# Attention logits in a ring of three PSUM banks instead of two, and a 16-bit SBUF target for the output stage's squares

## The reference

```
h = rms_norm(x) * (1 + scale) + shift              # modulation from silu(c) @ w_ada
q_a,k_a,v_a,gate_a, q_i,k_i,w_i, q_b,k_b,v_b,gate_b = split(h @ w_in)
score = sum_h relu(q_i . k_i) * w_i                # indexer: top 256 keys of each query
o_a = softmax(q_a . k_a over the chosen keys) v_a  # 8 heads, 2 key heads, width 64
o_b = retention(q_b, k_b, v_b, state)              # 4 heads of 128
y = rms_norm(concat(o_a silu(gate_a), norm(o_b) silu(gate_b)) @ w_out)
x = x + gate * y
```

## Time and profile before

| | |
|---|---|
| median of 3 runs | 1569.04 us (1568.35 to 1569.26) |
| the profiled execution's own time | 1566.93 us |
| its span in the profile | 1565.1 us |
| mean granted TensorE clock | 0.971 |
| busy: PE, DVE, ACT, POOL | 91%, 67%, 50%, 24% |
| first attention stages (layer 0, layer 1) | about 460 to 715 us, 1217 to 1470 us |

### The profile page before, as it was taken

The page is one execution under the profiler, slowest core; times in us unless marked ns, Lnnn a source line. Parts: engine busy times, 40 slices in busy tenths (PEclk is TensorE's granted clock), DMA queues, the critical chain, the costliest instruction groups (busy, mean ns, idle before and its releaser), DMA issues.

```text
span 1565.1 us, 24314 instructions
## 1 busy us (share of the span) xinstructions
PE 1422.0 (91%) x7591; PEld 1073.2 (69%) x7591; DVE 1046.1 (67%) x3026; ACT 787.0 (50%) x1916; POOL 383.4 (24%) x350
## 2 busy tenths in 40 slices
PE   6869999999999799889965899999999988988996
PEld 1745777777887567557855658778788755755785
DVE  0686998999985446441366779999999654654224
ACT  2545665665236455554333466666632555545422
POOL 2540333334321001001234212434433100100110
PEclk9899999999999999999987999999999999999998
DMA  9312343332221112113332111211112210211324
GB/s 334 94 57 63 89 122 121 113 114 75 70 69 50 32 34 84 52 53 105 111 109 70 36 38 33 56 49 46 57 53 83 60 40 31 67 54 54 104 79 161
DMA packets 125190, 122.04 MB, mean 78 GB/s; under 512 B 33256, under 2 KB 94024, under 8 KB 125064
## 3 DMA queue, kind: packets, MB, share of 16 engines
q1 hardware_dynamic: 125064, 120.49, 25.3%
HBM read 93.55 MB, written 26.90 MB: 77 GB/s over the span
## 4 chain that ended last, share of the span: by engine, by line
PE 53%; DVE 29%; ACT 6%; issue 6%; DMA 3%; POOL 2%; SPq 1%; DVEq 0%; ACTq 0%
PE proj L902 10%; PE proj L903 10%; PE proj L905 9%; PE turn L881 8%; PE logit L921 6%; DVE U L1529 5%; PE out_bank L946 4%; DMA U<-x_dram 2%; DVE by_cos_sin L1467 2%; DVE U L1723 2%; DVE by_cos_sin L1469 2%; DVE turned L1484 1%; DVE score L1503 1%; DVE probsT_more L1602 1%; ACT probsT_more L1209 1%
## 5 line engine op out<-in xcount | busy, mean ns | idle before, releaser
L902 PE MATMUL proj<-w_hi,h_hi 128*128 128x512 f32 (+2 forms) x1440 | 582.5, 405 | 2.2 <-ACT U L1145 1.4
L903 PE MATMUL proj<-w_lo,h_hi 128*128 128x512 f32 (+2 forms) x1440 | 541.0, 376 | 0.0
L905 PE MATMUL proj<-w_hi,h_lo 128*128 128x512 f32 (+2 forms) x1280 | 482.9, 377 | 0.0
L1347 POOL TENSOR_TENSOR w_lo<-w_raw,w_hi 128x512 fp32r<-128x512 f32 (+2 forms) x160 | 206.7, 1292 | 839.1 <-ACT w_hi L1101 839.1
L902 PEld LDWEIGHTS proj<-w_hi,h_hi 128*128 128x128 f32 x1440 | 276.8, 192 | 62.3 <-issue 23.1
L903 PEld LDWEIGHTS proj<-w_lo,h_hi 128*128 128x128 f32 x1440 | 277.5, 193 | 31.4
L905 PEld LDWEIGHTS proj<-w_hi,h_lo 128*128 128x128 f32 x1280 | 244.6, 191 | 37.4
L1529 DVE TENSOR_SCALAR_CACHE_REDUCE U<-score,cand 128x384 bf16<-128x384 f32 x310 | 222.6, 752 | 2.2
L921 PE MATMUL logit<-keys,queries 64*128 64x512 f32 (+4 forms) x592 | 142.5, 557 | 40.8 <-DVE row_max L1673 22.7
L1209 ACT ACTIVATE probsT_more<-turn 128x512 f32<-128x512 f32 (+3 forms) x156 | 73.3, 491 | 159.6 <-PE turn L881 127.4
L881 PE MATMUL turn<-ident,U 128*128 128x128 f32 x696 | 114.9, 294 | 28.5 <-DVE U L1723 13.8
(11 more groups left out here) (154 smaller groups left out, 2025.6 us busy)
## 6 DMA issues: line engine op xcount, KB each, us to landing
w_raw<-in_w_in_dram SPq DMA_DIRECT2D x80, 256.0 KB, 3.2
probsT_more<-in_w_ada_dram SPq DMA_DIRECT2D x64, 256.0 KB, 3.8
score<-mixed_dram SPq DMA_DIRECT2D x36, 256.0 KB, 2.8
U<-in_x_prompt_dram SPq DMA_DIRECT2D x16, 512.0 KB, 4.1
score<-in_w_ada_dram SPq DMA_DIRECT2D x32, 256.0 KB, 5.0
w_raw<-in_w_out_dram SPq DMA_DIRECT2D x32, 256.0 KB, 3.2
mixed_dram<-U SPq DMA_DIRECT2D x24, 192.0 KB, 2.1
gates_dram<-U SPq DMA_DIRECT2D x18, 256.0 KB, 2.1
```

The costliest lines, as they stand in the source:

```text
L902: nc.tensor.matmul(out, h_hi[:, k, tile], hi, start=(k == 0), stop=False)
L903: ins = nc.tensor.matmul(out, h_hi[:, k, tile], lo, start=False, stop=(t == SAMPLE and k == KT - 1))
L905: ins = nc.tensor.matmul(out, h_lo[:, k, tile], hi, start=False, stop=(k == KT - 1))
L1347: nc.gpsimd.tensor_tensor(w_lo[:, s % WS, 0:w], w_raw[:, n % RAWS, 0:w], w_hi[:, s % WS, 0:w].bitcast(F32), ALU.subtract).then_inc(w_lo_re ...
```

## The change

The attention logits get a list and a ring of their own, with three banks: the two logit banks and `spare`. Indexer and retention logits keep the ring of two. Since the rings share banks, TensorE gets waits where a stage changes from one to the other: before the first attention logit of a layer, for the last two keys of the ring of two and for the last modulation copy, and before the first searched indexer tile of layer 1, for the last three keys of the ring of three. `Ring` counts by the number of its banks. The squares of the output groups and of the new x go to `square_dump`, 512 bf16 columns of one slot of `rows` in SBUF; those of the input tiles still go to `spare`.

```diff
--- before.py
+++ after.py
@@ -310,7 +310,10 @@
 
 TURNS, LOGITS = plan_units()
 TURN_AT = {key: n for n, key in enumerate(TURNS)}
+ATT_LOGITS = [key for key in LOGITS if key[0] == "l" and kind(key[1]) == "att"]
+LOGITS = [key for key in LOGITS if key not in set(ATT_LOGITS)]
 LOGIT_AT = {key: n for n, key in enumerate(LOGITS)}
+ATT_LOGIT_AT = {key: n for n, key in enumerate(ATT_LOGITS)}
 PART_AT = {part: n for n, part in enumerate((g, p) for g in ATT_STEPS for p in range(len(att_parts(g))))}
 RB = 2
 RAWS = 3
@@ -367,27 +370,30 @@
     def __init__(self, banks, at, full, taken):
         self.banks, self.at, self.full, self.taken = banks, at, full, taken
 
+    def place(self, key):
+        return self.at[key] % len(self.banks), self.at[key] // len(self.banks)
+
     def bank(self, key):
-        return self.banks[self.at[key] % RB]
+        return self.banks[self.place(key)[0]]
 
     def wait_free(self, eng, key):
-        n = self.at[key]
-        if n >= RB:
-            eng.wait_ge(self.taken[n % RB], n // RB)
+        slot, turn = self.place(key)
+        if turn:
+            eng.wait_ge(self.taken[slot], turn)
 
     def wait_full(self, eng, key):
-        n = self.at[key]
-        eng.wait_ge(self.full[n % RB], n // RB + 1)
+        slot, turn = self.place(key)
+        eng.wait_ge(self.full[slot], turn + 1)
 
     def wait_taken(self, eng, key):
-        n = self.at[key]
-        eng.wait_ge(self.taken[n % RB], n // RB + 1)
+        slot, turn = self.place(key)
+        eng.wait_ge(self.taken[slot], turn + 1)
 
     def filled(self, ins, key):
-        ins.then_inc(self.full[self.at[key] % RB], 1)
+        ins.then_inc(self.full[self.place(key)[0]], 1)
 
     def take(self, ins, key):
-        ins.then_inc(self.taken[self.at[key] % RB], 1)
+        ins.then_inc(self.taken[self.place(key)[0]], 1)
 
 
 class Stores:
@@ -495,6 +501,7 @@
         gate_in = score[:, 2560:3072].rearrange("p (s n) -> p s n", s=2)
         att_out = score[:, 3072:3584].rearrange("p (s n) -> p s n", s=2)
 
+        square_dump = rows[:, 0, :].bitcast(BF16)[:, 0:512]
         relu = U[:, 4096:5120].rearrange("p (s n) -> p s n", s=2)
 
         xt = U[:, 0:2048].rearrange("p (s n) -> p s n", s=2)
@@ -565,6 +572,8 @@
         turn_taken = [sem(f"turn_taken{n}") for n in range(RB)]
         logit_full = [sem(f"logit_full{n}") for n in range(RB)]
         logit_taken = [sem(f"logit_taken{n}") for n in range(RB)]
+        att_full = [sem(f"att_full{n}") for n in range(3)]
+        att_taken = [sem(f"att_taken{n}") for n in range(3)]
         relu_used = sem("relu_used")
         neg_ready = sem("neg_ready")
         probs_ready = sem("probs_ready")
@@ -592,6 +601,11 @@
 
         turns = Ring(turn_banks, TURN_AT, turn_full, turn_taken)
         logits = Ring(logit_banks, LOGIT_AT, logit_full, logit_taken)
+        att_logits = Ring([*logit_banks, spare], ATT_LOGIT_AT, att_full, att_taken)
+
+        def ring_of(g):
+
+            return att_logits if kind(g) == "att" else logits
 
         def hidden_half(l, t, u):
 
@@ -638,7 +652,7 @@
                     t = lct(j)[2]
                     if kind(j) == "att" or t in SEARCHED:
                         held = valid_keys(t) if kind(j) == "idx" else blocks_of(t)[1] * P
-                        logits.wait_full(eng, ("l", j, 3, len(key_parts(held)) - 1))
+                        ring_of(j).wait_full(eng, ("l", j, 3, len(key_parts(held)) - 1))
 
         def raw_value(n):
 
@@ -912,13 +926,21 @@
                 k0 = blocks_of(t)[0] * P
                 parts = key_parts(valid_keys(t)) if kind(g) == "idx" else att_parts(g)
                 heads = dots_at(i, q)
+                ring = ring_of(g)
+                if heads[0] == (0, 0) and lct(g)[1:] == (ATT0, 0):
+                    for key in [k for k in LOGITS if k[1] < g][-RB:]:
+                        logits.wait_taken(pe, key)
+                    pe.wait_ge(ada_copied, len(ADA_GROUPS))
+                if heads[0] == (0, 0) and lct(g)[1:] == (0, SEARCHED[0]) and lct(g)[0]:
+                    for key in [k for k in ATT_LOGITS if k[1] < g][-3:]:
+                        att_logits.wait_taken(pe, key)
                 for h, p in heads:
-                    logits.wait_free(pe, ("l", g, h, p))
+                    ring.wait_free(pe, ("l", g, h, p))
                 for h, p in heads:
                     a, m = parts[p]
                     rows_ = slice(HD * (h % 2), HD * (h % 2) + HD)
                     key = ("l", g, h, p)
-                    logits.filled(nc.tensor.matmul(logits.bank(key)[:, 0:m], queries[rows_, HILO[g] % 2, h // 2, :],
+                    ring.filled(nc.tensor.matmul(ring.bank(key)[:, 0:m], queries[rows_, HILO[g] % 2, h // 2, :],
                                                    keys[rows_, k0 + a:k0 + a + m], start=True, stop=True), key)
 
             def turn_probs(n):
@@ -1083,12 +1105,12 @@
 
             squared = []
 
-            def square(src, total, signal, value):
+            def square(src, total, signal, value, dump):
 
 
                 if squared:
                     act.wait_ge(*squared[-1])
-                nc.scalar.activation(spare[:], src, ACT.Square, scale=D ** -0.5, accum_out=total).then_inc(signal, 1)
+                nc.scalar.activation(dump, src, ACT.Square, scale=D ** -0.5, accum_out=total).then_inc(signal, 1)
                 squared.append((signal, value))
 
             def split_weights(s):
@@ -1158,13 +1180,14 @@
                         if t:
                             act.wait_ge(x_new, l * NT + t)
                     nc.scalar.activation(dst, src[:], ACT.Copy)
-                    square(src[:], squares[:, t, 0, half:half + 1], proj_taken, g + 1)
+                    square(src[:], squares[:, t, 0, half:half + 1], proj_taken, g + 1, square_dump)
 
             def square_x(n):
 
                 t = n % NT
                 for u in (0, 1):
-                    square(xt[:, n % 2, u * 512:(u + 1) * 512], squares[:, t + 1, 1, u:u + 1], x_squared, 2 * n + u + 1)
+                    square(xt[:, n % 2, u * 512:(u + 1) * 512], squares[:, t + 1, 1, u:u + 1], x_squared, 2 * n + u + 1,
+                           spare[:] if n < NT else square_dump)
 
             def take_turn(g):
                 turns.wait_full(act, ("q", g))
@@ -1194,7 +1217,7 @@
                 if HILO[g] >= NT:
                     j = HILO_STEPS[HILO[g] - NT + 1]
                     n = valid_keys(SAMPLE) if kind(j) == "idx" else blocks_of(SAMPLE)[1] * P
-                    logits.wait_full(act, ("l", j, 3, len(key_parts(n)) - 1))
+                    ring_of(j).wait_full(act, ("l", j, 3, len(key_parts(n)) - 1))
                 turns.take(nc.scalar.activation(keys[:, SAMPLE_KEYS:SAMPLE_KEYS + PAST],
                                                 turns.bank(("cache", g))[:, 0:PAST], ACT.Copy), ("cache", g))
 
@@ -1422,8 +1445,8 @@
 
             def take(ring, ins, key):
                 ring.take(ins, key)
-                n = ring.at[key]
-                last[0] = (ring.taken[n % RB], n // RB + 1)
+                slot, turn = ring.place(key)
+                last[0] = (ring.taken[slot], turn + 1)
 
             def fence():
 
@@ -1669,9 +1692,9 @@
                         fence()
                     elif n >= 4:
                         turns.wait_full(dve, last_probs(n - 4))
-                    logits.wait_full(dve, key)
-                    take(logits, nc.vector.tensor_tensor_reduce(
-                        probs[n % 4][:, a:a + m], logits.bank(key)[:, 0:m], mask(t)[:, a:a + m], 1.0,
+                    att_logits.wait_full(dve, key)
+                    take(att_logits, nc.vector.tensor_tensor_reduce(
+                        probs[n % 4][:, a:a + m], att_logits.bank(key)[:, 0:m], mask(t)[:, a:a + m], 1.0,
                         row_max[:, n % 4, p - 1:p] if p else LOWEST, ALU.add, ALU.max, row_max[:, n % 4, p:p + 1]), key)
                     if p == len(parts) - 1:
                         fence()
```

## The result

The changed kernel takes 1555.44 us (median of 4 runs, 1554.35 to 1557.57), the kernel before beside it 1568.87 us (4 runs). The ratio is 0.9916, with a 95% interval of 0.9899 to 0.9933. I had said 1559.0, between 1554.5 and 1563.5. The profiled execution took 1554.35 us, with a span of 1552.6 us against 1565.1.

The account below looks back on a forecast made before the run. TensorE, busy 91% of the span, was taken as the bound, with time won only where it stands still. 1566.93 - 8.64 + 0.5 - 1.9 = 1556.9, plus 2.1 to the median: 1559.0 us, range 1554.5 to 1563.5.

Parts of the forecast that it names:

- The ring: Attention stages: twelve long logit waits each end 0.61 us earlier, 7.32 us; 8.64 us with shorter ones.
- the short waits: Two logit-pair waits per attention stage, shown as issue: their excess of 0.66 us a layer goes, 1.32 us in all.
- That the wait is one maximum shorter, because of VectorE's queue: Attention quarter 1: the pair no longer waits for VectorE's second maximum after the rotation, 0.61 us less per wait.
- The third bank is not what TensorE waits for: Rival, attention pairs: keys, queries or rotation hold them, the third bank gives 0; 1569.5 us, chance of no gain 0.05.
- the wait comes back elsewhere: Rival, after the attention pair: a held ScalarE eviction returns half of each 0.61 us; 1563.3 us, chance 0.10.
- Slower, by drops: Rival, attention waits: five more drops of TensorE's clock use up the gain, 1570.4 us; chance 0.04.
- The clock stays up: Rival, attention stages: all three drops of TensorE's clock go, 5.66 us gained, 1555.2 us; chance 0.13.
- The squares: Second output stage, layer 0: 7 x 3 squares on the chain cost 23 ns more each into SBUF, 0.5 us.
- The clock: Attention stages: one of TensorE's three drops to the 1.2 GHz level goes, 1.9 us gained.
- The gap of 2.1 us to the median: Whole kernel: median of the runs taken as 2.1 us above the profiled execution, raising 1556.9 to 1559.0 us.

Follow-up runs that it names:

- the second profile: Profile of the changed kernel run again with no edit: 1555.43 us, ratio 0.992 to the kernel before.

## Why the prediction was right, step by step

**The ring.** Its mechanism and size were right. I had 12 x 0.61 = 7.32 us; the twelve waits are shorter by 0.58 to 0.62 us each, and nothing takes it back: in the next pairs the distance to the kernel before stays what it was. The rest of the gain, 8.8 - 7.3 = 1.5 us, lies at the short waits and in the pairs next to them, where I had 1.32; one pair a layer that I had not counted showed 0.29 and 0.30 us (at 496.78 and 1253.50) and now shows 0.26. Sum 8.64 expected, 8.8 measured with the drops taken off. That only this, and not the squares, carries it is shown by the squares alone (ratio 1.0001) and by the ring with PSUM squares.

**That the wait is one maximum shorter, because of VectorE's queue.** Shown by the order: with the maxima ahead of the rotation, even two banks leave only one wait of 0.66 us a layer and four of 0.47 to 0.49.

**The rivals.** "The third bank is not what TensorE waits for" and "the wait comes back elsewhere" fell with the twelve rows. "Slower, by drops" fell: fewer drops came. "The clock stays up" did not happen in the profile, with two drops left and one in the second profile, but the medians lie next to its 1555.2. That is chance: other terms made up the difference (below).

**The squares.** This term failed in its sign. I charged 0.5 us, from a copy whose mean duration is 23 ns longer than a square's. The duration was indeed 28 ns longer where the source is SBUF, but the stage is 0.16 us shorter. The estimate of 613 ns for either target, from the Trainium skill ("ScalarE: Activation LUTs", section "What ACT_TABLE_LOAD costs"), would have given 0 here; that is nearer in the sum, though that formula has no term for source or destination, and the trace has 592 ns from PSUM and 630 from SBUF for a 16-bit SBUF target. The other remark that I took from that page of the Trainium skill, that PSUM is the destination of lower latency (it stands in the section "Step-by-step: what each stage is for"), fits the 602 ns against 630 of a single square from SBUF, but not the chain, which is 0.16 us shorter with SBUF.

**The clock.** I expected one drop fewer, 1.9 us. In the two profiles it was 3.1 us: one drop fewer, and the remaining two, after the longest waits, cost 1.1 and 1.4 us instead of 2.5. This is the term that was mis-sized. That it was one drop fewer is borne out by the count above, 2 to 4 with two banks and 1 to 2 with three, but which of these numbers one execution gets is chance. By the profiled executions' own times, 1566.93 - 1554.35 = 12.6 us: 8.8 of the ring, 3.1 of the clock, 0.16 of the squares, and 0.5 that was already there at the first attention pair.

**The gap of 2.1 us to the median** I took as fixed. It is not: the kernel after has its median 1.1 us above its profiled execution, and the kernel before gave medians of 1567.64, 1568.69 and 1569.62 us in three further series. The remaining 3.6 us between 1559.0 and 1555.4 are 1.0 of this gap, 1.2 of the clock, 0.7 of the squares, and 0.7 of the ring (0.16) and of what lay ahead of the first attention pair (0.5).

## What to carry to other kernels

When the busiest engine waits for a bank, ask what the engine that frees it did just before. Here a third bank cut each wait by one instruction (0.8%), while moving two VectorE instructions ahead of a rotation whose result TensorE needed only later took the waits away (1.8%). A list of waits can shrink by 7.5 us for some 1 us of gain, as with the own waits of matmuls that run side by side: check the start of the next work instead. Such a list also counts what an instruction shows that waits for nothing (0.25 us here), which cannot be won. And time between two fixed instructions, compared with a twin at full clock, separates what an edit gives from what TensorE's clock gives.

## What the runs showed that I had not expected

The granted clock drops after standstills of TensorE well below the 3.23 us of the longest: in the kernel before after 1.52 and 1.78 us, with two banks and own waits in attention even after one of 0.85 us (at 511.04; granted clock 1.00 up to 514 us, 0.50 in 514 to 516), though the same wait in the other layer, or in another execution of the same code, passes without. With three banks the longest wait of a layer was followed by one in 7 of 8 cases. Single runs of the kernel before lie between 1564.0 and 1573.6 us, and with 12 runs against 23 the interval of a ratio was still 0.12% to either side.

A logit matmul over 64 rows and 256 columns takes 0.70 us alone and 0.70 us as one of two. A ScalarE square with accumulator takes 592 ns (PSUM to bf16 SBUF), 594 (PSUM to PSUM), 602 (SBUF to PSUM) and 630 (SBUF to bf16 SBUF), and a chain of three is no longer for the last.
